# Expert rounds regrouped, transposes of gathered rows in two halves, final factors and the last gathers at other places

## The reference, cut to what matters

```python
def hier_moe(x, norm_g, router_g, router_g_b, router_e, router_e_b, exp_w1, exp_w3, exp_w2):
    xt = rms_norm(x, norm_g).reshape(n * t, D_MODEL)
    g_idx = jnp.argmax(g_logits, axis=-1)
    ...
    top_v, top_i = lax.top_k(e_sel, TOP_K_IN_GROUP)
    ...
    for g in range(N_GROUPS):
        h1 = jnp.einsum('td,edf->tef', xt, exp_w1[g])
        h3 = jnp.einsum('td,edf->tef', xt, exp_w3[g])
        act = jax.nn.silu(h1) * h3 * comb[:, g, :, None]
        out = out + jnp.einsum('tef,efd->td', act, exp_w2[g])
    return x + out.reshape(n, t, D_MODEL)
```

## Time and profile before

| what | value |
|---|---|
| three runs | 657.73, 661.57 and 661.98 us, median 661.57 us |
| the profiled execution | 659.6 us |
| its span in the profile | 657.8 us, 1.8 us less |
| mean granted clock of TensorE | 0.975 of full speed |
| TensorE busy | 608.8 us (93% of the span) |
| VectorE, ScalarE, GpSimd busy | 326.4, 186.4 and 83.1 us |
| read from and written to HBM | 172.85 MB and 15.61 MB |
| fetches of expert weights | 96 of 1 MB |

### The profile page before, as it was taken

The page is one execution under the profiler, slowest core; times in us unless marked ns, Lnnn a source line. Parts: engine busy times, 40 slices in busy tenths (PEclk is TensorE's granted clock), DMA queues, the critical chain, the costliest instruction groups (busy, mean ns, idle before and its releaser), DMA issues.

```text
span 657.8 us, 12077 instructions
## 1 busy us (share of the span) xinstructions
PE 608.8 (93%) x4950; PEld 484.5 (74%) x4950; DVE 326.4 (50%) x671; ACT 186.4 (28%) x319; POOL 83.1 (13%) x149
## 2 busy tenths in 40 slices
PE   8999999999999999998999999999997499898893
PEld 8999997577899999984778879555555265466552
DVE  5669799989643564676713156312221022112227
ACT  5523233245834334336003160111101000011013
POOL 1000000000002110000302211231111011111034
PEclk9999999999999999999899987999999799899998
DMA  8772210326545223659859778899999999999974
GB/s 325 287 290 86 108 66 2 132 87 201 183 146 183 84 109 130 256 198 377 322 221 385 293 277 331 353 400 419 418 420 419 421 420 420 418 419 421 418 275 193
DMA packets 35523, 179.46 MB, mean 273 GB/s; under 512 B 8967, under 2 KB 10407, under 8 KB 16645
## 3 DMA queue, kind: packets, MB, share of 16 engines
q1 hardware_dynamic: 26317, 163.19, 63.0%
q0 software_dynamic: 5600, 12.76, 5.0%
q10 hardware_dynamic: 3552, 2.75, 1.3%
HBM read 172.85 MB, written 15.61 MB: 286 GB/s over the span
## 4 chain that ended last, share of the span: by engine, by line
PE 68%; DMA 11%; SPq 8%; issue 5%; DVE 4%; ACT 2%; POOL 1%; DVEq 0%; ACTq 0%; POOLq 0%
PE ps L1843 13%; PE ps L1845 12%; PE ps L1844 12%; PE ps L2297 11%; PE ps L2326 6%; DMA w<-exp_w 5%; SPq L680 5%; PE ps L1839 4%; PE ps L1957 3%; SPq L689 3%; DMA q_rows<-q_s 2%; DMA raw<-weights 2%; PE ps L1914 1%; DMA qb<-q_rows 1%; DMA xe<-x_rows,g_idx 1%
## 5 line engine op out<-in xcount | busy, mean ns | idle before, releaser
L1843 PE MATMUL ps<-xH,w_h 128*128 128x260 f32 x480 | 138.3, 288 | 0.4 <-DVE xL L1461 0.3
L1845 PE MATMUL ps<-xL,w_h 128*128 128x260 f32 x480 | 135.6, 283 | 0.0
L1844 PE MATMUL ps<-xH,w_l 128*128 128x260 f32 x480 | 135.4, 282 | 0.0
L2297 PE MATMUL ps<-w,xeT 128*64 128x256 f32 (+2 forms) x1024 | 116.1, 388 | 10.4 <-DMA w<-exp_w 8.5
L2297 PEld LDWEIGHTS ps<-w,xeT 128*64 128x64 f32 (+2 forms) x1024 | 82.0, 139 | 47.9 <-issue 21.7
L1843 PEld LDWEIGHTS ps<-xH,w_h 128*128 128x128 f32 x480 | 90.3, 188 | 5.3 <-issue 4.6
L1844 PEld LDWEIGHTS ps<-xH,w_l 128*128 128x128 f32 x480 | 90.3, 188 | 0.3 <-issue 0.2
L1845 PEld LDWEIGHTS ps<-xL,w_h 128*128 128x128 f32 x480 | 90.4, 188 | 0.0
L2326 PE MATMUL ps<-w,aT 128*64 128x512 f32 (+2 forms) x256 | 61.8, 640 | 17.9 <-DVE aT L1732 12.1
L1142 DVE TENSOR_TENSOR w_l<-raw,w_h 128x2048 fp32r<-128x2048 f32 x27 | 61.8, 2289 | 28.4 <-ACT w_h L808 28.3
L808 ACT ACTIVATE w_h<-raw 128x2048 fp32r<-128x2048 f32 x27 | 51.6, 1910 | 21.9 <-PE ps L1845 18.6
(11 more groups left out here) (390 smaller groups left out, 895.1 us busy)
## 6 DMA issues: line engine op xcount, KB each, us to landing
w<-exp_w SPq DMA_DIRECT2D x96, 1024.0 KB, 24.0
raw<-weights SPq DMA_DIRECT2D x27, 1024.0 KB, 5.4
raw<-caches SPq DMA_DIRECT2D x16, 1024.0 KB, 6.2
qb<-q_rows POOLq DMA_DIRECT2D x4, 1024.0 KB, 7.4
yr<-y_rows SPq DMA_DIRECT2D x4, 1024.0 KB, 8.6
xT<-x_turned SPq DMA_DIRECT2D x4, 520.0 KB, 7.5
raw<-x_prompt SPq DMA_DIRECT2D x4, 512.0 KB, 12.4
x_rows<-x ACTq DMA_DIRECT2D x4, 512.0 KB
```

Source lines behind the costliest of these rows:

```text
L1843: pe.matmul(out, h1, h2, start=start, stop=False)
L1844: pe.matmul(out, l1, h2, start=False, stop=False)
L1845: return pe.matmul(out, h1, l2, start=False, stop=stop)
L2297: last = pe.matmul((mm[0][half, j, 0:FF], ta[1][half, 0:FF])[h], columns[:, k, half], w13[s][:, h, k, :], start=k == 0, stop=k == KT_D - 1)
```

## The change

It has four parts.

1. The string of rounds becomes PPPPQQSPPPPSP: 13 rounds, still 28 places: two S rounds fewer and one P round more. HEAVY has two places instead of four, MIDDLE two more, LIGHT the same eight. The two Q rounds follow each other as rounds 4 and 5. LATE becomes 12. The loop, its slots and the rule for the number of turns stay.
2. The eight transposes of a next round's rows are halved: four (into the first half of `tv`) ahead of the two transposes of `gated`, four behind them, in the rounds before the loop and the first round of a turn. On VectorE the copy of `aT` moves ahead of `columns_right` there.
3. GpSimd waits for the loop's last gathers behind its four additions and not ahead of them.
4. SyncE issues `fin_g` and `fin_gs` when the last loop round's `down` is done, ahead of its waits for the scatters, and not between the reads of `yr`.

```diff
-for kind in "PPPPSQSQSPPPSP":
+for kind in "PPPPQQSPPPPSP":
...
             for i, e in zip(LATE_SLOTS, which):
                 load_down(i, e)
 
+            wait(y_done, loops_n * 2 + LATE)
+            sp.dma_start(fin_g[:], a["final_norm_g"].rearrange("(o d) -> o d", o=1).broadcast_to([P, D])).then_inc(fg_in, 16)
+            sp.dma_start(fin_gs[0:N_PARTS], a["final_g_parts"]).then_inc(fg_in, 16)
             for i in range(ROWS):
...
                 sp.dma_start(yr[t][:], rows[t0:t0 + n]).then_inc(yr_in[t], 16)
-                if t == 1:
-                    sp.dma_start(fin_g[:], a["final_norm_g"].rearrange("(o d) -> o d", o=1).broadcast_to([P, D])).then_inc(fg_in, 16)
-                    sp.dma_start(fin_gs[0:N_PARTS], a["final_g_parts"]).then_inc(fg_in, 16)
...
                 gate_of(q, q % 2, of_slot[:, 0, q:q + 1], q >= 1)
+                act_columns_out(q, q >= 1)
                 if q + 1 < LATE:
                     columns_right(q + 1, (q + 1) % 2, q if q >= 1 else None)
                 else:
                     columns_right(LATE, 2, LATE)
-                act_columns_out(q, q >= 1)
                 rows_out(q, xe[q % ROWS], of_slot[:, 1, q:q + 1])
...
-            def turned_rows(tile):
+            def columns_of(tile, b):
 
                 rows = tile[:].rearrange("s (p k) -> s k p", k=KT_D)
-                for k in range(KT_D):
-                    last = turn(tv[k // 4][:, (k % 4) * P:(k % 4 + 1) * P], rows[:, k, :])
-                last.then_inc(xt_done, 1)
+                for k in range(4):
+                    last = turn(tv[b][:, k * P:(k + 1) * P], rows[:, 4 * b + k, :])
+                return last
...
-                    turned_rows(xe_late)
+                columns_of(following, 0)
                 act_columns(q, q >= 1)
+                columns_of(following, 1).then_inc(xt_done, 1)
                 down(q, slots_of(q), q >= 1)
...
-            for i in LOOP_ROWS:
-                wait(xe_landed[i], loops_n * 16 + 16 * (scattered(i, LATE) + 1))
             for t in range(4):
                 pool.wait_ge(yr_in[t], 16)
                 pool.tensor_tensor(x2[:, t, :], yr[t][:, 0, :], yr[t][:, 1, :], ALU.add).then_inc(y_pair, 1)
+            for i in LOOP_ROWS:
+                wait(xe_landed[i], loops_n * 16 + 16 * (scattered(i, LATE) + 1))
```

More of the change, by code:

```diff
@@ L1753, in _ @@
                 gate_of(it * 2 + LATE, LOOP_J[0], now[:, 0, 0:1])
+                act_columns_out(it * 2 + LATE)
                 columns_right(it * 2 + (LATE + 2), LOOP_J[1], it * 2 + LATE)
-                act_columns_out(it * 2 + LATE)
                 rows_out(it * 2 + LATE, xe[LOOP_ROWS[0]], now[:, 1, 0:1])
@@ L2269, in slot_lists @@
                 listed(ta[0], lambda n, i, j: hot_two[0:n, i, j].rearrange("p w c -> p (w c)"), lambda x: x.bitcast(F32))
-            def turned_rows(tile):
+            def columns_of(tile, b):
                 rows = tile[:].rearrange("s (p k) -> s k p", k=KT_D)
-                for k in range(KT_D):
-                    last = turn(tv[k // 4][:, (k % 4) * P:(k % 4 + 1) * P], rows[:, k, :])
-                last.then_inc(xt_done, 1)
+                for k in range(4):
+                    last = turn(tv[b][:, k * P:(k + 1) * P], rows[:, 4 * b + k, :])
+                return last
             def gathered_columns(i, gathers):
                 pe.wait_ge(xe_landed[i], 16 * gathers)
-                turned_rows(xe[i])
+                columns_of(xe[i], 0)
+                columns_of(xe[i], 1).then_inc(xt_done, 1)
             def hidden(q, j, loads, old=True, between=None, turned=None):
@@ L2338, in _ @@
                 hidden(q, q % 2, slots_of(q), q >= 2, slot_lists if q == 0 else None)
+                following = xe[(q + 1) % ROWS] if q + 1 < LATE else xe_late
                 if q + 1 < LATE:
-                    gathered_columns((q + 1) % ROWS, (q + 1) // ROWS + 1)
+                    pe.wait_ge(xe_landed[(q + 1) % ROWS], 16 * ((q + 1) // ROWS + 1))
                 else:
                     pe.wait_ge(late_in, 32)
-                    turned_rows(xe_late)
+                columns_of(following, 0)
                 act_columns(q, q >= 1)
+                columns_of(following, 1).then_inc(xt_done, 1)
                 down(q, slots_of(q), q >= 1)
@@ L2353, in _ @@
                 hidden(it * 2 + LATE, LOOP_J[0], slots[0:2], turned=(it * 2 + (LATE + 2), xeT[LOOP_J[0]]))
-                gathered_columns(LOOP_ROWS[1], it + ((LATE + 1) // ROWS + 1))
+                pe.wait_ge(xe_landed[LOOP_ROWS[1]], (it + ((LATE + 1) // ROWS + 1)) * 16)
+                columns_of(xe[LOOP_ROWS[1]], 0)
                 act_columns(it * 2 + LATE)
+                columns_of(xe[LOOP_ROWS[1]], 1).then_inc(xt_done, 1)
                 down(it * 2 + LATE, slots[0:2])
```

## The result

The changed kernel takes 697.02 us (median of 4 runs, 695.44 to 698.9), the kernel before 659.65 us (median of 4). The ratio is 1.057, with a 95% interval of 1.054 to 1.060: slower by 37 us. The forecast was 697 us, range 686 to 705. Run again later beside others it had 697.04 us.

A forecast was written before the change was run, and what follows sets the result against it. Expert weights bound the stage up to 567 us; then TensorE leads by a little. Late down at 672.5, plus 23.1 for the end, less 1.0, plus 1.8 around the span gave 696.4, taken as 697 us; range 686 to 705.

The forecast's parts named there:

- Second turn: In the loop: the third expert's 74 tokens exceed 64 places, so two more rounds, 17 against 16, and twelve more fetches.
- Round 5's w2: In the second Q round: w2 of place 15, the 33rd fetch, lands at 514.1, so round 5 loses 29 us.
- A round's transposes: In rounds before the loop: halving the transposes saves 0.35 us a round, bounds 0.6 and -0.3.
- Round 10's waits: At round 10's down: its 56th fetch might cause a wait of a microsecond or two; none counted.
- The loop: From the S round's start through the first turn: 15.28 and 12.98 us, each less 0.35, then 12.41.
- The gap: Between the turns: scatter, gather and transposes to the second turn's first hidden take 14.7 us, between 7.8 and 18.4.
- Clock: In the second turn's first round: TensorE restarts at the 1.2 GHz level, 1.8 us more, with 0 as other end.
- The end: From the late down to the span's end: 23.1 us becomes 1.0 shorter by moving GpSimd's wait and the factors' fetch.
- The figure: The whole time: 696.4 us for the profiled execution, 697 taken because the median before lay 2.0 above its own.
- the cheap line: Rival, between the turns: the gather takes the empty one's 2.1 us and no clock is lost; 690 us; chance 0.2.
- the dear line: Rival: gathers of 12.7 us, a wait with cold start in round 10, first jump back; 705 us; chance 0.14.
- One turn: Rival, in the loop: the third expert fits or its block isn't counted, fifteen rounds run; 657 us; chance 0.04.

The follow-up runs named there:

- run with the held addition: The new kernel with GpSimd's fourth addition held back until VectorE has done its first scaling (line 1789): 696.59 us.
- run with 60 tokens: The new kernel with 0.3 taken from expert 21's router bias, so that it has 60 tokens and fits its 64 places: 657.98 us, ratio 0.997.
- two orders of rounds: The new kernel with string PPPPQPQSPPPSP, a P round between the Q rounds, 701.67 us, beside the new kernel unchanged, 697.04 us.
- run with three turns: The new kernel with the number of loop turns set one higher, the third turn doing only unused work: 739.6 us.
- the one with the gather sooner: The new kernel with GpSimd's gather for the next turn's first round issued right after that round's scatter has landed: 689.95 us.

## Why the prediction was right

Point by point, with the prediction's figure first.

- *Second turn*: yes; 108 fetches and 17 rounds. The data alone switch it on and off, between 60 and 69 tokens.
- *Round 5's w2* at 514.1: its down started at 511.94. The idle time was 16.97 + 3.65 + 2.04 = 22.7 us, and the two halves of its hidden ran slow besides (6.30 and 6.45 us against 3.6), together 28 us where 29 were forecast. Behind it the prediction took 5.3 us to round 6, the slow down of the earlier trace rows; this down ran at full speed (3.64) and it was 3.6, so round 6 started at 515.51 and not 519.4.
- *A round's transposes*, 0.35 us: a P round took 437.40 - 425.17 = 12.23 us, and before 438.86 - 426.09 = 12.77, so 0.54, within the bound of 0.6:

```profile
426.09 7.08 PE L2297 MATMUL ps<-w,xeT 128*64 128x256 f32 x64
...
438.86 7.08 PE L2297 MATMUL ps<-w,xeT 128*64 128x256 f32 x64
```

  The term was too small because it was taken from the loop's second round. There 1.84 us pass from hidden to down; before the loop it is now 433.91 - 425.17 - 7.08 = 1.66.
- *Round 10's waits*, none counted: 0.88 + 1.45 + 1.14 = 3.5 us. The shorter rounds and the earlier round 6 brought TensorE ahead of the weights, which took most of it back: the S round started at 580.86, against 582.0. That these errors cancel to 1.1 us is in part luck.
- *The loop*: 14.94 and 12.60 us between starts, against 14.93 and 12.63. The 12.41 behind them is crossed only in the second turn, and it was 12.41 there.
- *The gap*, 14.7 us: 636.59 - 620.8 = 15.8, counted like the forecast from where the late round would start. The 3.1 to the gather held, the gather took 9.1 (9 taken); the step from the transposes to hidden was 3.47 and not 2.6, as the eight transposes also ran at half clock (1.97 us against 1.04). The error is of the clock's kind: its term counted only the first half of hidden.
- *Clock*: the first round of the turn took 651.17 - 636.59 = 14.6 us against 12.60 in the turn before: 2.0, not 1.8 (and 5.46 less half of 7.11 is 1.9).
- *The late down*: 672.71 against 672.5, the errors above cancelling (1.1 sooner at the S round, 1.1 later in the gap).
- *The end*, 1.0 us shorter: 0.3 us longer. This step failed. VectorE's wait of 0.97 us for GpSimd did go, and the second scaling gained 0.35 (1.28 us, where it took 1.63), but the first now starts just after GpSimd's fourth addition has begun, and takes 1.5 us more. Why it costs more to meet an addition at that moment is told at the end of this document. The run with the held addition gives 22.25, near the 22.1 of the forecast.
- *The figure*: the sum of 696.4 us stands for the profiled execution, which took 697.88; of the 1.5 between them 1.3 are the end. The 2.0 by which the median before lay above its profiled execution would have made 698.4 and not 697, and with a fourth run that median is 659.65, with nothing to add. That 697 and 697.02 agree to a tenth is luck. Not luck are the second turn, the gap within 1.1 us and the turn behind it within 0.2: each was read from a row.

GpSimd's fit in the Trainium skill, "DMA: Bandwidth & Descriptors", section "Anatomy of one DMA", would have put the gather at an estimated 2.1 us; it took 9.1 with 10 valid rows under a full queue, so the choice of the rows over the fit was right.

Of the rivals, the cheap line is refuted by the same row, and its argument, that only 10 rows are valid, by the gathers of no valid row that took 8.6 and 9.1 us. Of the dear line's three prices only the waits in round 10 came, 3.5 us, and without the slow down behind them (3.65 us); the gather took 9.1 and not 12.7. The jump back showed no price: TensorE started 0.04 us after the gather had landed. One turn is what the run with 60 tokens is: 658 us, where 657 was forecast, the down 2.6 us sooner than the rival's 631.0 and the end 2.9 longer than its 22.1, so that its figure too is good by cancelling.

Not settled: what parts 2 and 4 do to the whole time by themselves; they were never run apart.

## What to carry to other kernels

Where the amount of work is set by data, check a change of the buckets against the data first: a bucket that is 10 rows too small cost a loop turn of 40 us, while the round that it saved was worth nothing, as the fetches of the weights were the bound. Count, for each stage that waits, which number its fetch has in the queue and how much the engine still has to do behind it; here that gave the time of round 5's down to 2 us and 3 of the 4.6 us between two orders of rounds. A wait between loop turns that has never been crossed in a profile is priced from its parts (last write, scatter, gather, first use, restart at a low clock), and each part has a row. The gather's part is read from gathers that met as full a queue, not from one that met an idle one: 9 us against 2 here.

## What the runs showed of the hardware

GpSimd's additions and VectorE's scaling of two operands in SBUF do not run side by side: the one that has begun is finished first, and the other waits. In the new kernel the scaling at 682.31 starts 0.4 us after GpSimd's fourth addition, the second of the two merged above, has begun. By itself, in the timeline of GpSimd in a window inside it (so too the two of its kind below), it is:

```profile
681.92 2.35 POOL L2554 TENSOR_TENSOR x<-yr 128x1024 f32<-128x1024 f32 x1
```

The addition takes the 2.35 us of one that runs alone and ends at 684.27; the scaling ends 1.09 us behind it. Before, the scaling at 645.15 (its line stands with the end, above) met the end of the third addition (645.61) and ended 1.09 us behind that, and the fourth addition, which began while the scaling ran, took 1.0 us more than one alone:

```profile
645.57 3.34 POOL L2551 TENSOR_TENSOR x<-yr 128x1024 f32<-128x1024 f32 x1
```

In the run with three turns the scaling came 0.1 us before the end of the third addition. It was hardly held, and the fourth addition paid:

```profile
724.28 1.29 DVE L1789 SCALAR_TENSOR_TENSOR yo<-x,fin_ss,fin_g 128x1024 f32<-128x1024 f32 x1
```

```profile
724.50 3.29 POOL L2554 TENSOR_TENSOR x<-yr 128x1024 f32<-128x1024 f32 x1
```

It is the same in all fourteen profiles: each of the 20 scalings of 1024 columns that began more than 0.2 us before the end of a running addition was done 1.07 to 1.09 us behind that end, whether it had begun 0.5 or 2.2 us before it, and an addition that began while a scaling ran took 3.18 to 3.35 us. So an early start of the additions is worth what it saves in waits, less the rest of the addition that the scaling happens to meet: 0.5 us before, 2.0 in the new kernel. VectorE's additions, with one operand in PSUM, kept their 1.2 us in every run. The Trainium skill, "GPSIMD Engine Reference", section "Key points", says that the two engines share their interfaces to SBUF and contend where VectorE's instruction has two SBUF inputs; the runs agree, and show who pays.

How long a gather takes to land hung on the queue and hardly on its rows. Beside the weights, at a DMA share of 1.01 to 1.03, gathers of some 50 to 100 rows took 9.7 to 12.7 us, those of 10 rows 9.14 and 7.78 (the new kernel, and the one with the gather sooner), and those of no valid row 9.08 and 8.55; a gather of no valid row in a queue that had just run dry took 2.1.
